# Attention scores over all 128 rows, and norm, modulation and residual in one stage

## What is computed

```
mod = silu(c) @ ada_w[l] + ada_b[l]            # shift, scale, gate; twice per layer
h   = x * (1 + scale) + shift                  # modulation
y   = mixer(h)  or  ffn(h)  or  peer(h)
x   = layer_norm(ALPHA * x + gate * y) * g + b # ALPHA = (2 * DEPTH) ** 0.25
```

## Time and profile before

| | |
|---|---|
| median of 3 runs | 4222.34 us (4219.94 to 4237.76) |
| the profiled execution's own time | 4231.81 us |
| its span | 4230.0 us |
| PE busy | 3157.3 us (75%) |
| DVE busy | 2299.4 us (54%) |
| ACT busy | 1045.5 us (25%) |
| POOL busy | 931.3 us (22%) |
| mean granted clock | 0.903 |

### The profile page before, as it was taken

How to read it: one execution, slowest core, us unless ns; L and a number is a source line. 1 busy time by engine, 2 the same in 40 slices (tenths; PEclk the granted TensorE clock), 3 DMA queues, 4 the chain that set the end, 5 groups by cost and what they waited for, 6 DMA issues and landing times. The chain is left out here.

```text
span 4230.0 us, 36608 instructions
## 1 busy us (share of the span) xinstructions
PE 3157.3 (75%) x12012; PEld 1851.5 (44%) x12012; DVE 2299.4 (54%) x4802; ACT 1045.5 (25%) x2385; POOL 931.3 (22%) x804
## 2 busy tenths in 40 slices
PE   6768975987976868788777777777666564777776
PEld 1757934963834755233232232222264562322322
DVE  4456546746156348644755755555433659555554
ACT  1335423521232332111111111111232241111111
POOL 0000000000000011344444444444200023544442
PEclk9869997998986689999999999999987887999999
DMA  7214553545200112999999999999530034999996
GB/s 290 91 40 146 180 228 107 173 153 210 74 0 0 40 65 83 400 422 422 421 421 422 421 420 422 421 422 422 226 131 0 1 126 194 421 421 422 421 422 253
DMA packets 166459, 1052.88 MB, mean 249 GB/s; under 512 B 18333, under 2 KB 22173, under 8 KB 55345
## 3 DMA queue, kind: packets, MB, share of 16 engines
q0 software_dynamic: 110592, 805.36, 45.8%
q1 hardware_dynamic: 55728, 245.89, 16.4%
HBM read 1050.12 MB, written 1.05 MB: 249 GB/s over the span
## 5 line engine op out<-in xcount | busy, mean ns | idle before, releaser
L1806 PE MATMUL peer_fetch_summed<-peer_fetch_raw,peer_fetch_diag 128*128 128x512 f32 x3072 | 1447.1, 618 | 496.4 <-ACT peer_fetch_diag L1745 496.1
L1702 DVE CUSTOM_DVE_ANT_0 peer_fetch_raw<-peer_fetch_raw,peer_rows 128x1024 f32<-128x1024 f32 x768 | 940.3, 1225 | 850.8 <-DMA peer_fetch_raw<-in_peer_uv,peer_fetch_experts 850.3
L1806 PEld LDWEIGHTS peer_fetch_summed<-peer_fetch_raw,peer_fetch_diag 128*128 128x128 f32 x3072 | 569.7, 194 | 1364.3 <-ACT peer_fetch_diag L1745 772.1
L1624 POOL DMA_INDIRECT peer_fetch_raw<-in_peer_uv,peer_fetch_experts x768 | 854.9, 1113 | 1185.6 <-PE peer_fetch_summed L1806 1056.2
L1549 POOL TENSOR_TENSOR peer_keys_lo<-peer_pick_wq_raw,peer_keys_hi 128x1024 fp32r<-128x1024 f32 x32 | 76.2, 2387 | 2055.2 <-ACT peer_keys_hi L1508 2055.2
L1736 ACT ACTIVATE peer_fetch_gelu<-peer_fetch_score 128x2 f32<-128x2 f32 x384 | 78.1, 203 | 1628.1 <-DVE peer_fetch_score L1702 1628.1
L1745 ACT ACTIVATE peer_fetch_diag<-all_constants,peer_fetch_gelu 128x128 f32<-128x128 f32 x768 | 260.0, 386 | 0.7
L130 PE MATMUL ffn_up_acc<-first_h_hi,ffn_up_hi 128*128 128x256 f32 x704 | 201.7, 287 | 35.8 <-DVE ffn_up_lo L650 35.8
L130 PE MATMUL ffn_up_acc<-first_h_lo,ffn_up_hi 128*128 128x256 f32 x704 | 201.3, 286 | 0.0
L130 PE MATMUL ffn_up_acc<-first_h_hi,ffn_up_lo 128*128 128x256 f32 x704 | 201.1, 286 | 0.0
L458 PE MATMUL mod_acc<-mod_weights,mod_act_c 128*1 128x512 f32 (+1 forms) x288 | 137.9, 624 | 44.3 <-DMA mod_weights<-in_ada_w 31.7
(11 more groups left out here) (483 smaller groups left out, 4781.5 us busy)
## 6 DMA issues: line engine op xcount, KB each, us to landing
mod_weights<-in_ada_w SPq DMA_DIRECT2D x48, 1024.0 KB, 7.5
in_up_raw<-in_w_up SPq DMA_DIRECT2D x88, 512.0 KB, 4.2
mod_weights<-in_w_mod SPq DMA_DIRECT2D x24, 1024.0 KB, 6.2
peer_fetch_next_raw<-in_w_mod SPq DMA_DIRECT2D x24, 1024.0 KB, 8.9
ffn_down_raw<-in_w_down SPq DMA_DIRECT2D x32, 704.0 KB, 5.8
peer_pick_wq_raw<-in_peer_wq SPq DMA_DIRECT2D x32, 512.0 KB, 3.7
peer_fetch_raw<-in_peer_uv,peer_fetch_experts POOLq DMA_INDIRECT x768, 18.6
in_in_raw<-in_ab_w_in SPq DMA_DIRECT2D x17, 512.0 KB, 3.8
```

The source lines that it names most:

```text
L1624: nc.gpsimd.indirect_dma_start(raw[:, n % ring].rearrange("p c d -> p (c d)"), None, uv_rows, bass.IndirectOffsetOnAxis(index[:, i, e:e + ...
L1702: nc.vector.tensor_tensor_reduce(raw[:, n % ring, 0, :], raw[:, n % ring, 0, :], rows[:, i, :], 1.0, 0.0, ALU.mult, ALU.add, score[:, i, e ...
L1806: ins = nc.tensor.matmul(summed[:, i % 2, half, :], diag[:, n % dring, :], raw[:, n % ring, 1, half * 512:(half + 1) * 512], start=(e == 0 ...
```

## The change

Four edits come together. (1) In attention DVE first zeroes a tile "wide" of two copies of the key columns and copies each key head into its own 64 rows of its own copy; the score products then use all 128 rows of q and of wide, so that the other key head's rows meet zeros, and 512 key columns are one product instead of two. (2) The closing projections no longer write z: DVE adds the gated sum straight into x (join), two chunks behind its own weight splitting (one in the FFN's). (3) layer_norm works on x in place, and takes modulate's work: per chunk DVE multiplies by the root, makes h with the norm's gain and bias folded into the modulation's (two small tiles made at its start), and makes h_lo two chunks behind; ACT makes h_hi and then the new x with ALPHA folded into gain and bias. The weights ahead are fetched from its start. (4) The norms ahead of the two later modulation stages move behind them, and the one at the start of the second block handles the context stream's modulation beside the norm ("beside").

```
-        total = sum(n for n, _ in segments)
+        total = KD if into else sum(n for n, _ in segments)
...
+                if into:
+                    dve.sem_inc(s_taken, banks)
+                def lo(m, bank, turn):
-                each_chunk(dve, 0, total, banks, body)
+                def join(m):
+                    x, gate = into
+                    dve.wait_ge(s_used, m * pieces + 4 + pieces)
+                    for n in range(t // T):
+                        half = slice(n * T, (n + 1) * T)
+                        ins = nc.vector.scalar_tensor_tensor(x[:, m, half], acc[:, m % banks, half], gate[:, m, n:n + 1],
+                                                             x[:, m, half], ALU.mult, ALU.add)
+                    ins.then_inc(s_taken, 1)
+                if into:
+                    lead = banks // 2
+                    for m in range(total + lead):
+                        if m < total:
+                            lo(m, m % banks, m // banks)
+                        if m >= lead:
+                            join(m - lead)
+                else:
+                    each_chunk(dve, 0, total, banks, lo)
...
-                act.sem_inc(s_taken, banks)
+                if not into:
+                    act.sem_inc(s_taken, banks)
...
+                if into:
+                    for m in range(total):
+                        hi(m, m % banks, m // banks)
+                    return
...
-def layer_norm(nc, name, x, z, sq, t, gain, bias, mean_of_d, residual=True):
+def layer_norm(nc, name, x, sq, gain, bias, mean_of_d, then=None):
...
+            if then and then.ahead:
+                @block.sync
+                def _(sp):
+                    then.ahead.start(sp)
...
-                    if residual:
-                        pe.wait_ge(s_added, k + 1)
-                    ins = nc.tensor.matmul(ps_mean[:, 0:t], mean_of_d, z[:, k, :], start=(k == 0), stop=(k == KD - 1))
+                    ins = nc.tensor.matmul(ps_mean[:, 0:t], mean_of_d, x[:, k, :], start=(k == 0), stop=(k == KD - 1))
...
-                if residual:
-                    for k in range(KD):
-                        nc.vector.tensor_tensor(z[:, k, :], z[:, k, :], x[:, k, :], ALU.add).then_inc(s_added, 1)
+                if then:
+                    folded = Steps(dve, s_folded)
+                    folded.done(nc.vector.tensor_scalar(own_gain[:], gain, ALPHA, None, ALU.mult))
+                    folded.done(nc.vector.tensor_scalar(own_bias[:], bias, ALPHA, None, ALU.mult))
+                    for i, c in enumerate(then.cols):
+                        scale = then.mods[:, then.shift + KD:then.shift + 2 * KD, c]
+                        folded.done(nc.vector.tensor_tensor(next_gain[:, i, :], gain, scale, ALU.mult))
+                        folded.link(nc.vector.tensor_tensor(next_bias[:, i, :], bias, scale, ALU.mult))
+                        folded.link(nc.vector.tensor_tensor(next_bias[:, i, :], next_bias[:, i, :],
+                                                            then.mods[:, then.shift:then.shift + KD, c], ALU.add))
+                    if then.beside:
+                        other, c = then.beside
+                        left = slice(0, at)
+                        for k in range(KD):
+                            nc.vector.tensor_scalar(then.h[:, k, left], other[:, k, :], then.mods[:, then.shift + KD + k, c:c + 1],
+                                                    then.mods[:, then.shift + k, c:c + 1], ALU.mult, ALU.add).then_inc(s_other, 1)
                 dve.wait_ge(s_mean, 1)
                 for k in range(KD):
-                    nc.vector.tensor_tensor(z[:, k, :], z[:, k, :], ps_mean[:, 0:t], ALU.subtract).then_inc(s_centred, 1)
+                    nc.vector.tensor_tensor(x[:, k, :], x[:, k, :], ps_mean[:, 0:t], ALU.subtract).then_inc(s_centred, 1)
+                if then and then.beside:
+                    for k in range(KD):
+                        dve.wait_ge(s_other_hi, k + 1)
+                        nc.vector.tensor_tensor(then.pair[1][:, k, left], then.h[:, k, left], then.pair[0][:, k, left].bitcast(F32),
+                                                ALU.subtract)
+                    nc.vector.tensor_scalar(other, other, ALPHA, None, ALU.mult)
                 dve.wait_ge(s_var, 1)
                 step.link(nc.vector.tensor_scalar(rstd[:], ps_var[:, 0:t], LN_EPS, None, ALU.add))
                 step.link(nc.vector.reciprocal(rstd[:], rstd[:]))
                 dve.wait_ge(s_root, 1)
+                def lo(k):
+                    dve.wait_ge(s_hi, k + 1)
+                    nc.vector.tensor_tensor(then.pair[1][:, k, mine], then.h[:, k, mine], then.pair[0][:, k, mine].bitcast(F32),
+                                            ALU.subtract)
                 for k in range(KD):
-                    nc.vector.tensor_tensor(z[:, k, :], z[:, k, :], rstd[:], ALU.mult).then_inc(s_scaled, 1)
+                    nc.vector.tensor_tensor(x[:, k, :], x[:, k, :], rstd[:], ALU.mult).then_inc(s_scaled, 1)
+                    if then:
+                        dve.wait_ge(s_scaled, k + 1)
+                        for i in range(n):
+                            part = slice(i * T, (i + 1) * T)
+                            nc.vector.tensor_scalar(then.h[:, k, at + i * T:at + (i + 1) * T], x[:, k, part], next_gain[:, i, k:k + 1],
+                                                    next_bias[:, i, k:k + 1], ALU.mult, ALU.add).then_inc(s_h, 1)
+                        if then.pair and k >= 2:
+                            lo(k - 2)
+                if then and then.pair:
+                    lo(KD - 2)
+                    lo(KD - 1)
 
+                if then and then.beside:
+                    for k in range(KD):
+                        act.wait_ge(s_other, k + 1)
+                        nc.scalar.activation(then.pair[0][:, k, 0:at], then.h[:, k, 0:at], ACT.Copy).then_inc(s_other_hi, 1)
                 for k in range(KD):
                     act.wait_ge(s_centred, k + 1)
...
                 for k in range(KD):
-                    act.wait_ge(s_scaled, k + 1)
-                    nc.scalar.activation(x[:, k, :], z[:, k, :], ACT.Identity, bias=bias[:, k:k + 1],
-                                         scale=gain[:, k:k + 1])
+                    if then and then.pair:
+                        act.wait_ge(s_h, n * (k + 1))
+                        nc.scalar.activation(then.pair[0][:, k, mine], then.h[:, k, mine], ACT.Copy).then_inc(s_hi, 1)
+                    elif then:
+                        act.wait_ge(s_h, n * (k + 1))
+                    else:
+                        act.wait_ge(s_scaled, k + 1)
+                    scale, shift = (own_gain, own_bias) if then else (gain, bias)
+                    nc.scalar.activation(x[:, k, :], x[:, k, :], ACT.Identity, bias=shift[:, k:k + 1], scale=scale[:, k:k + 1])
...
+        wide = st.sb("wide", [P, 2, keys.shape[1]])
+        s_zero, s_wide = st.sem("zero"), st.sem("wide")
...
-                    rows = slice(g * A_DIM, (g + 1) * A_DIM)
+                    if n == 0:
+                        pe.wait_ge(s_wide, 2)
                     if n >= 2:
                         pe.wait_ge(s_exp, EXPS * (n - 1))
                     for c in range(pair):
-                        at = 0
-                        for kt in ks:
-                            w = kt.shape[1]
-                            ins = nc.tensor.matmul(scores[:, n % 2, c, at:at + w], q(first + c)[rows], kt[rows],
-                                                   start=True, stop=True)
-                            at += w
+                        ins = nc.tensor.matmul(scores[:, n % 2, c, 0:ks], q(first + c), wide[:, g, 0:ks], start=True, stop=True)
...
+                nc.vector.memset(wide[:], 0.0).then_inc(s_zero, 1)
+                dve.wait_ge(s_zero, 1)
+                for g in range(2):
+                    rows = slice(g * A_DIM, (g + 1) * A_DIM)
+                    nc.vector.tensor_copy(wide[rows, g, :], keys[rows]).then_inc(s_wide, 1)
...
             modulate(nc, "h00", h, pair, x, mods, 0, (0,), ahead)
-            even_mixer(nc, d, ahead, pair, z, mods, vec, con)
-        layer_norm(nc, "ln00", x, z, h, T, *ln(0, 0), con("mean_of_d"))
+            even_mixer(nc, d, ahead, pair, x, mods, vec, con)
         with Stage(nc, "in01") as st:
             ahead = Ahead(nc, st, "up", d["w_up"][0])
-            modulate(nc, "h01", h, pair, x, mods, 3 * KD, (0,), ahead)
-        layer_norm(nc, "ln01", x, z, h, T, *ln(0, 1), con("mean_of_d"))
+            layer_norm(nc, "ln00", x, h, *ln(0, 0), con("mean_of_d"), Next(h, pair, mods, 3 * KD, (0,), ahead))
         modulation(nc, "mod1", c, d["ada_w"][1], ada_b(1), mods, con("ident"))
-        modulate(nc, "h10", h, pair, x, mods, 0, (0,))
-        pool_mixer(nc, "pool", h, d["pool_w"], vec("pool_scale"), d["inv_count"], z, mods[:, 2 * KD:3 * KD, :], x)
```

(12 more changed lines are left out.)

88 lines of the change are left out of this document (43 added, 45 removed).

## The result

The changed kernel takes 4173.9 us (median of 4 runs, 4169.15 to 4178.95) where the kernel before, on the same chip, takes 4225.9 (4 runs, 4219.94 to 4237.76). The ratio is 0.9876, with a 95% interval of 0.9856 to 0.9896: faster, by 52 us. 4172 was forecast, with a range of 4153 to 4203. The profiled execution took 4177.4 us, with a span of 4175.6, 54.4 shorter than that of before (4230.0).

A forecast was written before the change was run, and what follows sets the result against it. No engine bounds the whole; PE at half clock bounds the second attention. The profiled 4231.8 us less 29.9 (attention) and 24.1 (norms) is 4177.8, from the median 4168.3; 4172 chosen, own range 4154 to 4190, with rivals 4153 to 4203.

The forecast's parts named there:

- The clock follows the rows: Attention score products: using all 128 rows instead of 64, even with zeros, lifts PE's clock from 1.2 to 2.4 GHz.
- rival (a): Both attentions: clock stays at 1.2 GHz, only the norms gain, total time 4198 to 4208 us; chance 0.13.
- The second attention: Clock rises some 10 us in; masked items 5.25 us apart, unmasked 2.7; saves 30.4, costs 1.7, net 28.7 us.
- The first attention: Clock rises late if at all: 2.1 us saved, 0.9 spent on zeroing, net 1.2 us.
- The norms: All seven norms with their modulations, fused or moved: 24.1 us saved in sum.
- the tail at 256 tokens: Norm from root products to x's scaling: 12.24 us becomes one DVE pass of 9.0, saving 3.2 us each.
- the clock of ln10's mean products: Norm ln10: mean products taken at the high clock's 3.72 us, the norm saving 3.2 us.
- The slow mean behind the two modulation stages: Moved norms ln01, ln11: mean products start at low clock, taking 6.75 and 6.8 us instead of about 3.72.
- ln20 and ln11: Norms of the second block: ln20 saves 3.9 us with the residual's lead, ln11 saves 4.5 us.
- ln21: Norm over 512 tokens without residual: 19.04 us becomes 16.0, saving 3.1 us.
- The closing projections: DVE's additions in 40 chunks fit in its idle time, so they cost nothing and give nothing.
- Rival (c): Closing projections: the additions starve PE, costing 68 to about 100 us, total time 4270 us; chance 0.03.

The follow-up runs named there:

- rows64: Changed kernel with score products over only the 64 rows of their key head, still all keys in one product: 4221.4 us.
- two_products: Changed kernel with all 128 rows but each score product split into pieces of at most 256 keys: 4176.3 us.
- norm_only: Changed kernel with the old attention put back (64 rows, one product per key piece): 4209.3 us, ratio 0.9957 to the kernel before.
- after_again: The changed kernel itself, unaltered, measured and traced once more: 4175.7 us, ratio 0.9852 to the kernel before.
- warm: Changed kernel with throwaway PE products ahead of attentions and ln10, key tile zeroed by GpSimd, one key copy on ACT: 4163.2 us.
- join_three: Changed kernel with two more DVE additions into scratch behind each real one in the closing projections, last chunks excepted: 4171.7 us, ratio 0.9872.

## Why the prediction was right, point by point

**The clock follows the rows: right.** It is the step on which most hung, and rows64 against two_products shows it. The 0.13 given to rival (a) is settled against it.

**The second attention, 28.7 net: 32.6 came.** The interval of 5.25 us was 5.15 to 5.19, the 2.7 was 2.71, the rise came 9.5 us in for my 10, and the fourth to the last scores shrank by 29.9 for my 30.4. In that sum one term was wrong: the two intervals of transition were put at 8.6 us "by the same two ratios", which give 7.9, and they took 10.6 (1346.13 to 1356.69), with the wait of 2.09 us for ACT and the stretch at 0.50 behind it. The other items made it up. The opening cost 2.1 (from the rope's end to the first scores 2.42 in place of 0.30) for my 1.7. What was missed is the drain: I left it at its time, and from the last scores to the stage's end it fell from 18.75 us to 14.55, for part of it had still been at 1.2 GHz. Rival (a)'s 0.3 us per masked item through fewer weight loads is not to be seen: rows64, with one product where norm_only has two, takes the same 115.1 us without its 2.1 us of opening.

**The first attention, 1.2 net: 2.3,** and in after_again the stage took 31.4 in place of 33.1 us with the same code. A stage that the clock reaches halfway is not sized better than that.

**The norms, 24.1: 21.1 in the marks, 19.4 in the runs of norm_only.** The run per chunk was right: 8.96 us for 9.0, and 512 tokens gave 3.2 (from the variance's end to the rows' products 24.26 and 21.08) for 3.1. Two terms of the sum were mis-sized. The first is the tail at 256 tokens: 3.2 taken, 2.1 to 2.3 found (ln00 from 333.41 to 348.86 and from 332.81 to 346.19; ln30 from 3432.22 to 3443.81, 11.6, and from 3379.75 to 3389.08, 9.3). I had measured the pattern on ln00 alone, whose boundary holds a semaphore clearing, the 2.98 idle ahead of 341.93. I let that vanish with the boundary. It goes by how many semaphores have been used, and stands now behind the fused stage, as the 1.57 ahead of 346.19. The second is the clock of ln10's mean products: I gave them 3.7, they took 6.62 where before they took 3.69, and the pool's own took 0.9 more; the stretch lost 1.7 in place of winning 3.2. warm shows that it is the level, and that PE kept busy holds it. Before, with 3.64 us of the same idle time, it was up, and none of the ten other traces without filling repeats that: the 3.69 that I counted from was the lucky case, and what decided it stays open.

The slow mean behind the two modulation stages came about as forecast: 6.11 us for ln01 and 5.74 for ln11, for 6.75 and 6.8. A stage of modulation ends with 48 products over one row (two rows in mod20), and both times the level fell while they ran: the granted clock was 1.00 from 600 to 622 and 0.50 from 626.4 to 628.3. In mod1:

```profile
623.71 3.38 PE L550 MATMUL mod_cols<-all_constants,mod_rows 1*128 1x1 f32 x48 [0.68 <-ACT mod_rows L558]
```

Against that ln20 and ln11 gave 4 us more than forecast and ln01 1.2. In it are 1.6 from ln20's mean at 7.11 for 8.73, about 1.2 from the clearing that no longer lies ahead of it, and 1.7 from ln11's mean before the change, which I took to be 3.7 as in ln00 and which was 5.41.

**ln21 gave 1.7 for 3.1.** Its products' stage begins 1.9 us behind the last h_lo (3030.04) in place of 0.5:

```profile
3031.97 1.06 ACT L272 ACTIVATE gla_k_hi<-mix_in_raw 128x1024 fp32r<-128x1024 f32 x1 [2.36 <-PEq L248]
```

The row names PE's sequencer, which came last; ahead of it the clearing of semaphores at L55 ran from 3030.3 to 3031.6. So the missing 1.4 us are the same term as in ln00: a clearing that the prediction didn't move along.

**The closing projections, nothing: right,** by join_three, and by their own lengths: from the first product to the last 24.8 (ab_out), 65.1, 64.9 (the FFNs'), 46.1 and 25.2 us, where they took 25.1, 65.4, 64.9, 45.9 and 25.0. Rival (c) rested on them.

**The run.** 4177.8 from the profiled execution, where the profiled one took 4177.4; 4168.3 from the median, 4172 chosen, and 4173.9 came. That it is so near is partly luck: attention 5 us above its terms, norms 3 to 5 below.
